# The attention matmuls of 32 and 64 rows in the first block become matmuls of 128 rows

## The chip, the cores and the metric

The kernel runs on one core of a Trainium2 chip. The metric is the device time of one launch in microseconds (us). Before the change three runs gave 2588.17, 2590.54 and 2590.59 us, a median of 2590.54 us.

## The reference, cut to what matters

The reference is a two-block network on 512 tokens of width 1024. The first block mixes three branches; the one that matters here is a sparse attention with 16 query heads of size 64 in 4 key/value groups (4 heads share the keys and values of a group). It has three parts, each with its own gate:

```
s_c = einsum('bghsd,bgnd->bghsn', qh, kc) * scale      # compressed keys: 31 blocks of 32 tokens
o_cmp = einsum('bghsn,bgnd->bghsd', softmax(s_c), vc)  # compressed values
s  = einsum(q, selected keys) * scale                  # 16 blocks can be selected, there are 8: all are
sw = einsum(q, window keys) * scale                    # window 512: all earlier tokens
o  = g0 * o_cmp + g1 * softmax(s) @ v_slc + g2 * softmax(sw) @ v_win
```

`kc` and `vc` come from a small two-layer network over blocks of keys and values. All is float32. The second block (two layers of another attention and a retention) is not touched.

## The kernel before, in words

**Precision.** The matmuls here take operands of the type `F32R`, which are rounded when they are written. So each operand is held in two parts, a rounded "hi" and the rest "lo", and a product is hi\*hi + hi\*lo + lo\*hi: three matmuls that add into one PSUM bank. ScalarE (ACT) writes hi parts, VectorE (DVE) or GpSimd (POOL) the lo parts. Weights stream from HBM in slabs of 8 tiles (128x128), which ACT rounds (`w_hi`) and POOL subtracts (`w_lo`).

**Orders.** Every engine walks the same Python program (`walk`), in which each engine's class implements only its own steps; a step that an engine does not have is `nothing`. So each engine's order of instructions is fixed when the program is written, and semaphore waits join them. Nothing is planned by cost.

**The stage of the change.** The attention is done in 32 sub-units, `SUBS` (L1613): pair of groups `gp` (2), block `i` of 128 queries (4), pair of heads `pp` (2), and `odd` (2), which says which group of the pair is meant. The head size is 64, so two groups lie in one tile of 128 partitions: the even group in rows 0 to 63 and the odd one in rows 64 to 127. The loop in `walk` runs 34 rounds. In round u it weaves, by fixed ratios (`weave`):

- `scores(u)`: four score products (`qk`, head h and branch br), 128\*(i+1) keys wide. DVE takes each out of its bank with the mask and the row minimum (`least`), ACT does the exponentials (`exps`), DVE and POOL the weights.
- `cmp_scores`: the compressed scores and their softmax, once for each block of queries.
- `values`: two rounds behind the scores, the transposed weights (`turn`), split by ACT (`pt_hi`) and DVE (`pt_lo`), then the products with the values (`times`). At a sub-unit's end `cmp_times` adds the compressed part to the same bank, and `out_high`, `out_add`, `out_split` take the result out into `Yhi` and `Ylo`.
- a filler of ordinary products with streamed weights: first the second pair's keys, values and queries (`groups(1)`), then a gate (`branch_gates`).

Six PSUM banks (`spots`) go round among these parts in order of release, two are the filler's.

**The two pairs.** In `qk`, the keys of a group stand in `KS` as 128 rows: the hi part in the group's own 64 rows and the lo part in the other 64. `twice` lets ACT copy the 64 rows of the hi queries into both halves of `QQ`. The first matmul, `QQ` with `KS`, has 128 rows and gives q_hi\*k_hi + q_hi\*k_lo. The second takes the group's own 64 rows of `Ylo` and of `KS` and adds q_lo\*k_hi. `KS` is what streams, and the queries are the loaded weights. In `cmp_times`, the compressed values of a group stand in 32 rows of `vc`, hi beside lo in its 128 columns; two matmuls of 32 rows each take them with the hi and with the lo part of the compressed weights (`ct_hi`, `ct_lo`, each 64 rows: 32 for each group). A row of the trace for line L1714 is a matmul of `mm`, for L1939 an ACT copy or activation of `put`, for L2233 a DVE two-operand instruction; the tiles tell which.

Of the kernel before, what the change touches and what calls it, by code (L numbers as in the profile page):

```python
# [31 lines left out]
R0 = 72  # L32
# [61 lines left out]
def f(ap):  # L94
    return ap.bitcast(F32)
# [76 lines left out]
def program(nc, A, out):  # L172
# [46 lines left out]
    vc = at("vc", R0 + 134, [64, 2, 128], F32R)  # L219
# [8 lines left out]
    Yhi = at("Yhi", R0, [128, KT, 512], F32R)  # L228
    Ylo = at("Ylo", R0 + 16, [128, KT, 512], F32R)
# [13 lines left out]
    QQ = [at(f"QQ{i}", 32 + i, [128, 2, 128], F32R) for i in range(2)]  # L243
# [5 lines left out]
    ct_hi = [at(f"ct_hi{i}", R0 + 130 + 2 * i, [64, 256], F32R) for i in range(2)]  # L249
    ct_lo = [at(f"ct_lo{i}", R0 + 131 + 2 * i, [64, 256], F32R) for i in range(2)]  # L250
    ov = [at(f"ov{i}", 34 + i, [128, 2, 128]) for i in range(2)]
# [120 lines left out]
    class Order:  # L372
# [536 lines left out]
        def cmp_turned(self, gp, i, pp):  # L909
# [3 lines left out]
            self.low(("ct", v), b, banks[b][0:64, 0:256], ct_hi[v % 2][:, :], ct_lo[v % 2][:, :],  # L913
# [796 lines left out]
    class Pe(Order):  # L1710
# [103 lines left out]
        def qk(self, u, n, b, bank_free):  # L1814
            gp, i, pp, odd = SUBS[u]
            h, br = n // 2, n % 2
            width, rows, j = 128 * (i + 1), slice(64 * odd, 64 * odd + 64), 4 * gp + 2 * pp + h
            self.wait_ge(act_nsa.by("twice", u), dve_kqv.by("k", gp, br), bank_free)
            self.mm(banks[b][:, 0:width], QQ[u % 2][:, h, :], KS[gp][odd][:, br, 0:width], True, False)
            self.wait_ge(dve_kqv.by("q", j))  # L1820
            self.mm(banks[b][:, 0:width], Ylo[rows, j, 128 * i:128 * i + 128], KS[gp][odd][rows, br, 0:width], False, True).then_inc(
                *scored(u, n))
# [18 lines left out]
        def cmp_times(self, u, v, ob):  # L1841
            gp, i, pp, odd = SUBS[u]
            rows, o = slice(32 * odd, 32 * odd + 32), banks[ob][:, 0:256]
            self.wait_ge(act_nsa.by("high", "ct", v), dve_cmp.by("value", 3))
            self.mm(o, vc[rows, gp, :], ct_hi[v % 2][rows, :], False, False)
            self.wait_ge(dve_nsa.by("low", "ct", v))
            names = [("out", u)] + [("ct", v)] * odd
            self.mm(o, vc[rows, gp, :], ct_lo[v % 2][rows, :], False, True).then_inc(*valued.named(*names))
# [86 lines left out]
    class Act(Order):  # L1935
# [109 lines left out]
        def twice(self, u, spare_free):  # L2045
            gp, i, pp, odd = SUBS[u]
            j = 4 * gp + 2 * pp
            src = Yhi[64 * odd:64 * odd + 64, j:j + 2, 128 * i:128 * i + 128]
            self.wait_ge(act_kqv.by("q", j + 1), dve_kqv.by("q", j + 1), scored.by(u - 2, 3) if u > 1 else None, spare_free)
            for y in range(2):  # L2050
                ins = self.put(QQ[u % 2][64 * y:64 * y + 64, :, :], src)
# [177 lines left out]
    class Dve(Order):  # L2229
# [97 lines left out]
        def cmp_zero(self):  # L2327
# [665 lines left out]
```

## Time and profile before

| what | value |
|---|---|
| median of three runs | 2590.54 us |
| profiled execution, its own time | 2593.51 us |
| its span, first to last instruction | 2591.7 us |
| PE (TensorE) busy | 2564.2 us, 99% |
| DVE busy | 1157.5 us, 45% |
| ACT busy | 1045.2 us, 40% |
| POOL busy | 1135.2 us, 44% |
| mean granted TensorE clock | 0.994 |
| the attention stage of the change | about 309.6 to 589 us of the span |
| DMA | 250.47 MB, mean 97 GB/s |

A row of the timeline is the start in us, the length in us, the engine, the line, and what was written from what (out<-in). For matmuls "64\*128" is the number of rows (partitions that are summed over) by the columns of the loaded weights, and "64x512" the rows by the streamed columns. A matmul's length is longer than its share of the engine, because matmuls are pipelined: what one costs is the distance from its start to the next one's start. PEld are the weight loads, which can overlap PE. In a wait the engine named behind `<-` released it.

### The profile page before, as it was taken

To read this page: it belongs to the slowest core of one execution; us is meant where nothing else is said; L and a number is where in the kernel's file an instruction comes from. 1 tells how busy PE (TensorE), PEld (TensorE's weight loads), DVE (VectorE), ACT (ScalarE), POOL (GpSimd) and SP (SyncE) were. 2 spreads that over 40 slices of the span, in tenths; PEclk is the share of its full clock that TensorE was granted. 3 is DMA by queue.
4 is the path that set the end of the run, shared out by engine and by line. 5 is a ranking of instruction groups with operands and counts; after the bars stand their busy time and mean duration, and the time that the engine had idled before them with its cause. 6 is when DMAs were issued, how large, how long until landed. Compare 5 with 4: busy or idle time off the path is not lost.

```text
span 2591.7 us, 33239 instructions
## 1 busy us (share of the span) xinstructions
PE 2564.2 (99%) x13376; PEld 2170.9 (84%) x13376; DVE 1157.5 (45%) x2373; ACT 1045.2 (40%) x2006; POOL 1135.2 (44%) x663
## 2 busy tenths in 40 slices
PE   8999999999999999999999999999999999999998
PEld 8888877778888888889888888888898888888887
DVE  6572466556432694101333354542142345544313
ACT  3462376763234433223443333333243333333322
POOL 3354344444445455445344444444444444444342
PEclk9999999999999999999999999999999999999999
DMA  5133210105533354223222222222222222222222
GB/s 189 66 102 105 72 33 25 34 25 195 195 106 138 109 192 167 96 95 105 78 82 82 82 80 83 86 86 98 98 99 88 83 84 79 88 82 83 96 94 87
DMA packets 71769, 250.47 MB, mean 97 GB/s; under 512 B 7872, under 2 KB 12736, under 8 KB 71232
## 3 DMA queue, kind: packets, MB, share of 16 engines
q1 hardware_dynamic: 71616, 248.35, 28.4%
q8 instruction: 106, 1.74, 0.3%
q14 instruction: 47, 0.39, 0.0%
HBM read 246.22 MB, written 2.10 MB: 96 GB/s over the span
## 4 chain that ended last, share of the span: by engine, by line
PE 93%; DVE 4%; ACT 2%; DMA 0%; issue 0%; POOL 0%; DVEq 0%; SPq 0%
PE bank L1714 91%; PE bank L1724 3%; DVE XC L2241 1%; DVE rk_lo L2233 0%; DVE Ylo L2233 0%; DVE sq L2233 0%; ACT TR L1939 0%; ACT w_hi L1939 0%; DVE nt L2233 0%; DMA w_raw<-in_wa 0%; DVE Hlo L2233 0%; DVE nB L2233 0%; ACT Hhi L1939 0%; DMA XR<-in_x 0%; DVE blkk L2237 0%
## 5 line engine op out<-in xcount | busy, mean ns | idle before, releaser
L2769 POOL TENSOR_TENSOR w_lo<-w_raw,w_hi 128x1024 fp32r<-128x1024 f32 (+1 forms) x398 | 949.6, 2390 | 1137.7 <-ACT w_hi L1939 1137.3
L1714 PE MATMUL bank<-Hhi,w_hi 128*128 128x512 f32 (+1 forms) x2144 | 844.0, 394 | 1.4 <-DVE XC L2241 1.3
L1714 PE MATMUL bank<-Hlo,w_hi 128*128 128x512 f32 (+1 forms) x2144 | 825.0, 385 | 2.2 <-DVE Hlo L2233 0.8
L1714 PE MATMUL bank<-Hhi,w_lo 128*128 128x512 f32 (+1 forms) x2144 | 824.2, 384 | 0.0
L1939 ACT ACTIVATE w_hi<-w_raw 128x1024 fp32r<-128x1024 f32 (+1 forms) x398 | 408.0, 1029 | 163.1 <-DMA w_raw<-in_wa 118.1
L1714 PEld LDWEIGHTS bank<-Hhi,w_lo 128*128 128x128 f32 x2144 | 404.5, 189 | 81.3
L1714 PEld LDWEIGHTS bank<-Hhi,w_hi 128*128 128x128 f32 x2144 | 405.1, 189 | 79.8 <-issue 5.3
L1714 PEld LDWEIGHTS bank<-Hlo,w_hi 128*128 128x128 f32 x2144 | 405.5, 189 | 72.3 <-DVE Hlo L2233 3.0
L1714 PE MATMUL bank<-w_hi,Hhi 128*128 128x256 f32 (+2 forms) x384 | 117.6, 306 | 0.0
L1714 PE MATMUL bank<-w_hi,Hlo 128*128 128x256 f32 (+2 forms) x384 | 116.0, 302 | 0.0
L1714 PE MATMUL bank<-w_lo,Hhi 128*128 128x256 f32 (+2 forms) x384 | 115.9, 302 | 0.0
L2794 POOL TENSOR_SCALAR PP<-PP,small 128x128 f32<-128x128 f32 (+3 forms) x128 | 66.1, 536 | 105.5 <-DVE small L2233 105.1
L2506 DVE CUSTOM_DVE_ANT_0 wm<-wm,c 128x1024 f32<-128x1024 f32 x48 | 78.9, 1647 | 9.5 <-DMA wm<-in_w_ada 9.3
L1714 PEld LDWEIGHTS bank<-w_hi,Hhi 128*128 128x128 f32 x384 | 73.0, 190 | 4.4
L1714 PE MATMUL bank<-Fhi,w_hi 128*128 128x512 f32 (+1 forms) x220 | 76.5, 348 | 0.0
L2476 DVE CUSTOM_DVE_ANT_0 PP<-bank,tri 128x128 f32<-128x128 f32 (+3 forms) x128 | 60.5, 487 | 35.7 <-PE bank L1714 34.9
L1714 PE MATMUL bank<-Flo,w_hi 128*128 128x512 f32 (+1 forms) x220 | 76.2, 347 | 0.0
L1714 PE MATMUL bank<-Fhi,w_lo 128*128 128x512 f32 (+1 forms) x220 | 76.2, 347 | 0.0
L1714 PEld LDWEIGHTS bank<-w_lo,Hhi 128*128 128x128 f32 x384 | 73.1, 190 | 3.1
L1939 ACT ACTIVATE PP<-PP,small 128x128 f32<-128x128 f32 (+3 forms) x128 | 70.6, 554 | 11.8 <-DVE small L2476 10.9
L1714 PE MATMUL bank<-Ylo,w_hi 128*128 128x512 f32 x192 | 74.8, 390 | 0.4 <-DVE Ylo L2233 0.4
L1714 PEld LDWEIGHTS bank<-w_hi,Hlo 128*128 128x128 f32 x384 | 73.1, 190 | 2.4
(355 smaller groups left out, 4264.6 us busy)
## 6 DMA issues: line engine op xcount, KB each, us to landing
w_raw<-in_wb SPq DMA_DIRECT2D x211, 512.0 KB, 3.4
w_raw<-in_wa SPq DMA_DIRECT2D x174, 512.0 KB, 3.4
wm<-in_w_ada SPq DMA_DIRECT2D x48, 512.0 KB, 4.4
wa_raw<-in_wb SPq DMA_DIRECT2D x5, 512.0 KB, 6.0
XR<-in_x SPq DMA_DIRECT2D x4, 512.0 KB, 6.5
w1k<-in_w1k SPq DMA_DIRECT2D x1, 2048.0 KB, 12.8
w1v<-in_w1v SPq DMA_DIRECT2D x1, 2048.0 KB, 17.7
XR<-in_x SPq DMA_DIRECT2D x1, 2048.0 KB, 8.3
```

Of the source, the lines that this page charges most:

```text
L1714: return self.e.matmul(o, lhs, rhs, start=start, stop=stop)
L1724: return self.e.transpose(o, i, ident[0:n, 0:n])
L1939: return self.e.activation(o, a, func, **kw)
L2241: return self.e.scalar_tensor_tensor(out=o, in0=a, scalar=s, in1=b, op0=op0, op1=op1)
L2476: self.e.tensor_tensor_reduce(PP[slot][:, n // 2, n % 2, 0:width], banks[b][:, 0:width], tri[:, 512 - width:512], -.125, 3e38, ALU.add, AL ...
L2506: self.e.tensor_tensor_reduce(x, x, cc[l][:, :], .5, 0., ALU.mult, ALU.add, mod[:, l, n:n + 1]).then_inc(*dve_mod("row", l, n))
L2769: self.e.tensor_tensor(x.lo[:, k:k + n, :], x.raw[:, k:k + n, :], f(x.hi[:, k:k + n, :]), ALU.subtract).then_inc(*w_rest(s, k))
L2794: self.e.tensor_scalar(p, p, r[:, n:n + 1], 1., ALU.mult, ALU.mult).then_inc(*pool_nsa("p", u, n))
```

## The change: what it does

- `QQ` gets a second plane: `twice` now copies the hi and the lo rests of the queries (`Y2` is `Yhi` and `Ylo` as one tile), each into both halves, with the same two ACT instructions, each twice as long in elements. The second matmul of `qk` takes `QQ[.., 1, ..]` with all 128 rows of `KS`, so it adds q_lo\*k_hi + q_lo\*k_lo.
- `ct_hi` and `ct_lo` become the two halves (rows 0 to 63 and 64 to 127) of one tile `ct`. `vc` becomes 128 rows for each group: hi and lo values in the group's 32 rows and again 64 rows below, zero elsewhere. `cmp_times` is one matmul of 128 rows, which waits for both parts of `ct`.
- `cmp_zero` clears `vc` too (one memset more), and `cmp_values` copies each group's 32 rows to their second place (four copies more).
- `ov`, `vc`, `QQ` and `ct` move in SBUF; to make room the program asks for 2048 bytes of dynamic DMA scratch in place of the default.

```diff
-    vc = at("vc", R0 + 134, [64, 2, 128], F32R)
+    vc = at("vc", R0 + 136, [128, 2, 2, 128], F32R)
...
-    Yhi = at("Yhi", R0, [128, KT, 512], F32R)
-    Ylo = at("Ylo", R0 + 16, [128, KT, 512], F32R)
+    Y2 = at("Y2", R0, [128, 2, KT, 512], F32R)
+    Yhi, Ylo = Y2[:, 0, :, :], Y2[:, 1, :, :]
...
-    QQ = [at(f"QQ{i}", 32 + i, [128, 2, 128], F32R) for i in range(2)]
+    QQ = [at(f"QQ{i}", 32 + 2 * i, [128, 2, 2, 128], F32R) for i in range(2)]
...
-    ct_hi = [at(f"ct_hi{i}", R0 + 130 + 2 * i, [64, 256], F32R) for i in range(2)]
-    ct_lo = [at(f"ct_lo{i}", R0 + 131 + 2 * i, [64, 256], F32R) for i in range(2)]
-    ov = [at(f"ov{i}", 34 + i, [128, 2, 128]) for i in range(2)]
+    ct = [at(f"ct{i}", R0 + 130 + i, [128, 256], F32R) for i in range(2)]
+    ov = [at(f"ov{i}", R0 + 132 + i, [128, 2, 128]) for i in range(2)]
...
         def qk(self, u, n, b, bank_free):
             gp, i, pp, odd = SUBS[u]
-            h, br = n // 2, n % 2
-            width, rows, j = 128 * (i + 1), slice(64 * odd, 64 * odd + 64), 4 * gp + 2 * pp + h
+            h, br, width = n // 2, n % 2, 128 * (i + 1)
             self.wait_ge(act_nsa.by("twice", u), dve_kqv.by("k", gp, br), bank_free)
-            self.mm(banks[b][:, 0:width], QQ[u % 2][:, h, :], KS[gp][odd][:, br, 0:width], True, False)
-            self.wait_ge(dve_kqv.by("q", j))
-            self.mm(banks[b][:, 0:width], Ylo[rows, j, 128 * i:128 * i + 128], KS[gp][odd][rows, br, 0:width], False, True).then_inc(
-                *scored(u, n))
+            self.mm(banks[b][:, 0:width], QQ[u % 2][:, 0, h, :], KS[gp][odd][:, br, 0:width], True, False)
+            self.mm(banks[b][:, 0:width], QQ[u % 2][:, 1, h, :], KS[gp][odd][:, br, 0:width], False, True).then_inc(*scored(u, n))
...
         def cmp_times(self, u, v, ob):
             gp, i, pp, odd = SUBS[u]
-            rows, o = slice(32 * odd, 32 * odd + 32), banks[ob][:, 0:256]
-            self.wait_ge(act_nsa.by("high", "ct", v), dve_cmp.by("value", 3))
-            self.mm(o, vc[rows, gp, :], ct_hi[v % 2][rows, :], False, False)
-            self.wait_ge(dve_nsa.by("low", "ct", v))
             names = [("out", u)] + [("ct", v)] * odd
-            self.mm(o, vc[rows, gp, :], ct_lo[v % 2][rows, :], False, True).then_inc(*valued.named(*names))
+            self.wait_ge(act_nsa.by("high", "ct", v), dve_nsa.by("low", "ct", v), dve_cmp.by("value", 3))
+            self.mm(banks[ob][:, 0:256], vc[:, gp, odd, :], ct[v % 2][:, :], False, True).then_inc(*valued.named(*names))
...
-            src = Yhi[64 * odd:64 * odd + 64, j:j + 2, 128 * i:128 * i + 128]
+            src = Y2[64 * odd:64 * odd + 64, :, j:j + 2, 128 * i:128 * i + 128]
             self.wait_ge(act_kqv.by("q", j + 1), dve_kqv.by("q", j + 1), scored.by(u - 2, 3) if u > 1 else None, spare_free)
             for y in range(2):
-                ins = self.put(QQ[u % 2][64 * y:64 * y + 64, :, :], src)
+                ins = self.put(QQ[u % 2][64 * y:64 * y + 64, :, :, :], src)
...
         def cmp_zero(self):
+            self.e.memset(f(vc[:, :, :, :]), 0.0)
             self.e.memset(f(kc[:, :, :]), 0.0).then_inc(*dve_cmp("zero"))
...
             for g in range(4):
-                dst, o = vc[32 * (g % 2):32 * (g % 2) + 32, g // 2, :], banks[b][0:32, 64 * g:64 * g + 64]
+                a, o = 32 * (g % 2), banks[b][0:32, 64 * g:64 * g + 64]
+                dst = vc[a:a + 32, g // 2, g % 2, :]
                 self.e.tensor_copy(dst[:, 0:64], o).then_inc(*dve_cmp("value high", g))
                 self.wait_ge(dve_cmp.now())
-                self.tt(dst[:, 64:128], o, f(dst[:, 0:64]), ALU.subtract).then_inc(*dve_cmp("value", g))
+                self.tt(dst[:, 64:128], o, f(dst[:, 0:64]), ALU.subtract).then_inc(*dve_cmp("value low", g))
+                self.wait_ge(dve_cmp.now())
+                self.e.tensor_copy(vc[64 + a:96 + a, g // 2, g % 2, :], dst).then_inc(*dve_cmp("value", g))
...
-    nc = _bacc.Bacc("TRN2", target_bir_lowering=False, num_devices=1)
+    nc = _bacc.Bacc("TRN2", target_bir_lowering=False, num_devices=1, dynamic_dma_scratch_size=2048)
```

## Rows read from the trace of the kernel before

**Rows 1.** The page: busy time of the engines, and the DMA queue.

```profile
PE 2564.2 (99%) x13376; PEld 2170.9 (84%) x13376; DVE 1157.5 (45%) x2373; ACT 1045.2 (40%) x2006; POOL 1135.2 (44%) x663
...
q1 hardware_dynamic: 71616, 248.35, 28.4%
```

**Rows 2.** Stretches: from:to length, busy us of PE, PEld, DVE, ACT, POOL, clock, DMA.

```profile
309.60:394.89 85.29, 85.29 (x466) 65.36 (x464) 53.79 (x181) 63.80 (x172) 39.16 (x58) 1.00 0.11 38
394.89:464.33 69.44, 69.44 (x381) 52.32 (x379) 43.66 (x132) 48.40 (x125) 28.85 (x44) 1.00 0.08 24
464.33:495.22 30.89, 30.89 (x152) 22.53 (x151) 17.59 (x61) 23.20 (x63) 14.05 (x21) 1.00 0.11 36
495.22:589.00 93.78, 93.44 (x499) 68.88 (x499) 55.27 (x143) 62.71 (x144) 37.43 (x46) 1.00 0.10 34
```

**Rows 3.** All waits of PE from 300 to 592 us: total, times, longest.

```profile
PE bank L1714 <- DVE pt_lo L2233: 0.3, 1, 0.3
```

**Rows 4.** PE's timeline, 395 to 404 us.

```profile
395.60 0.49 PE L1714 MATMUL bank<-KS,QQ 128*128 128x512 f32 x1
396.02 0.50 PE L1714 MATMUL bank<-KS,Ylo 64*128 64x512 f32 x1
396.45 0.33 PE L1714 MATMUL bank<-kc,Yhi 128*128 128x128 f32 x1
...
397.47 0.40 PE L1714 MATMUL bank<-Hhi,w_lo 128*128 128x512 f32 x1
397.70 0.39 PE L1714 MATMUL bank<-KS,QQ 128*128 128x512 f32 x1
...
402.29 0.28 PE L1714 MATMUL bank<-pt_hi,VS 128*128 128x256 f32 x1
402.41 0.28 PE L1714 MATMUL bank<-pt_lo,VS 128*128 128x256 f32 x1
402.62 0.38 PE L1714 MATMUL bank<-ct_hi,vc 32*128 32x256 f32 x1
402.85 0.27 PE L1714 MATMUL bank<-ct_lo,vc 32*128 32x256 f32 x1
...
403.39 0.39 PE L1714 MATMUL bank<-Hlo,w_hi 128*128 128x512 f32 x1
```

**Rows 5.** PE's timeline, 445 to 446 us: a narrow score pair and what follows it.

```profile
445.45 0.33 PE L1714 MATMUL bank<-KS,QQ 128*128 128x128 f32 x1
...
445.96 0.33 PE L1724 MATMUL bank<-ident,PP 128*128 128x128 f32 x1
```

**Rows 6.** Weight loads' timeline, 399 to 401 us.

```profile
399.93 0.18 PEld L1714 LDWEIGHTS bank<-KS,Ylo 64*128 64x128 f32 x1 [0.26 <-issue]
400.36 0.19 PEld L1714 LDWEIGHTS bank<-kc,Yhi 128*128 128x128 f32 x1 [0.25 <-issue]
```

**Rows 7.** ACT's groups by shape, 309.6 to 589 us: xcount, busy us, mean ns, idle before.

```profile
L1939 ACT ACTIVATE QQ<-Yhi 64x256 fp32r<-64x256 f32 x60 | 24.8, 413 | 1.1 <-issue 0.3
L1939 ACT ACTIVATE PP<-PP,small 128x512 f32<-128x512 f32 x32 | 22.8, 715 | 2.4 <-DVE small L2476 2.2
...
L1939 ACT ACTIVATE PP<-PP,small 128x256 f32<-128x256 f32 x32 | 16.0, 500 | 3.5 <-DVE small L2476 2.9
```

**Rows 8.** ACT's longest waits, 309.6 to 589 us: total, times, longest.

```profile
ACT pt_hi L1939 <- PE bank L1724: 27.8, 27, 2.7
ACT PP L1939 <- DVE small L2476: 10.9, 18, 1.3
...
ACT C L1939 <- DVE C L2233: 9.2, 6, 2.8
```

**Rows 9.** DVE's timeline, 98 to 108 us.

```profile
101.96 0.20 DVE L2349 CAST vc<-bank 32x64 fp32r<-32x64 f32 x1
...
105.53 0.81 DVE L2238 TENSOR_SCALAR XC<-bank,par 128x512 f32<-128x512 f32 x1 [1.64 <-PE bank L1714]
```

**Rows 10.** A stretch at a lower granted clock, columns as in rows 2.

```profile
1231.80:1242.00 10.20, 10.20 (x48) 10.20 (x48) 6.07 (x15) 4.39 (x10) 3.28 (x4) 0.50 0.01 4
```

More of the change, by code:

```diff
@@ L912, in cmp_turned @@
             v = 2 * (4 * gp + i) + pp
-            self.low(("ct", v), b, banks[b][0:64, 0:256], ct_hi[v % 2][:, :], ct_lo[v % 2][:, :],
+            self.low(("ct", v), b, banks[b][0:64, 0:256], ct[v % 2][0:64, :], ct[v % 2][64:128, :],
                      turned_.by("ct", v), valued.by("ct", v - 2) if v > 1 else None)
@@ L2345, in cmp_values @@
         def cmp_values(self, b, bank_free):
-            self.wait_ge(cmp_sums.by("value"), act_norm.by("h", "first", KT - 1, 1), pool_norm.by("rest", "first", KT - 1, 1))
+            self.wait_ge(cmp_sums.by("value"), dve_cmp.by("zero"), act_norm.by("h", "first", KT - 1, 1), pool_norm.by("rest", "first", KT - 1, 1))
             for g in range(4):
-                dst, o = vc[32 * (g % 2):32 * (g % 2) + 32, g // 2, :], banks[b][0:32, 64 * g:64 * g + 64]
+                a, o = 32 * (g % 2), banks[b][0:32, 64 * g:64 * g + 64]
+                dst = vc[a:a + 32, g // 2, g % 2, :]
                 self.e.tensor_copy(dst[:, 0:64], o).then_inc(*dve_cmp("value high", g))
                 self.wait_ge(dve_cmp.now())
-                self.tt(dst[:, 64:128], o, f(dst[:, 0:64]), ALU.subtract).then_inc(*dve_cmp("value", g))
+                self.tt(dst[:, 64:128], o, f(dst[:, 0:64]), ALU.subtract).then_inc(*dve_cmp("value low", g))
+                self.wait_ge(dve_cmp.now())
+                self.e.tensor_copy(vc[64 + a:96 + a, g // 2, g % 2, :], dst).then_inc(*dve_cmp("value", g))
         def conv(self, j, o, done):
```

## The prediction

> **What bounds the kernel now.** I began with the page's busy times: PE is busy 2564.2 of 2591.7 us, the next engine 45% [rows 1]. Whatever shortens PE's own work shortens the kernel, as long as another engine doesn't take over. So the second view was the stretches of the attention stage, 309.6 to 589 us. In each PE is busy all the time, ACT 63.8 of 85.3, 48.4 of 69.4, 23.2 of 30.9 and 62.7 of 93.8 us, DVE less than ACT, POOL less than half [rows 2]. PE's waits in the stage come to 0.3 us in all [rows 3]. The reader is to see two things: PE's stream is what the stage lasts, and ACT, at 70 to 75% of it, is the next bound and not far off.
>
> The third view was PE's timeline, where a matmul's cost is the distance between starts. A 512-column matmul of 128 rows costs 0.23 us (397.47 to 397.70), a 256-column one 0.12 us (402.29 to 402.41) [rows 4]. A score pair at 512 columns (`QQ`, then `Ylo` with 64 rows) costs 396.45 - 395.60 = 0.85 us, where two plain ones would take 0.46. The weight loads show why: the load for the 64-row matmul starts 0.26 us late, at its matmul's own start, and the next 128-row load is again 0.25 us late [rows 6]. Loads usually run under the matmul before. Here, with a change in the number of rows, each load waits until the array is through, on the way in and on the way out.
>
> **The change part by part, on PE.**
>
> *Score pairs at 256 to 512 columns.* 0.85 - 0.46 = 0.39 us each. I take the same for 256 and 384 columns, since what is lost is the hidden load and not time by column. There are 32 sub-units of four pairs, and three of four blocks of queries are this wide: 96 x 0.39 = 37.4 us.
>
> *Score pairs at 128 columns.* They take 445.96 - 445.45 = 0.51 us [rows 5]. Plain ones cannot cost more than a 256-column one (0.12), nor less than half of it (0.06), so the saving lies between 0.27 and 0.39 us. I take 0.27, because a weight load takes longer than 128 columns stream, and so sets the pace: 32 x 0.27 = 8.6 us.
>
> *Compressed values.* From `pt_lo` at 402.41 to `Hlo` at 403.39 are 0.98 us [rows 4]. With one 128-row matmul of 256 columns there would be 0.12 + 0.12 + 0.23 = 0.47. That saves 0.51 us, 32 times: 16.3 us. Of it 0.12 us is the matmul that goes, the rest the late loads.
>
> PE's work shrinks by 37.4 + 8.6 + 16.3 = 62.3 us. All of it lies on the path, for now.
>
> **On ACT.** `twice` copies 64 x 512 elements where it copied 64 x 256, at 413 ns. Such a copy isn't in the trace at that shape. Exponentials, also SBUF to SBUF, take 715 ns at 512 and 500 at 256 elements per partition [rows 7], so 256 more cost 215 ns. The bounds are 0 (if the fixed part were all) and 413 ns (if it were proportional). I take 215, as the nearest rows are the same engine and the same memory. In the four stretches there are 22, 16, 8 and 14 such copies, 60 in all [rows 7]: 12.9 us more for ACT. Queued behind a longer `twice` are `pt_hi` and the exponentials.
>
> **Which engine ends a stretch then.** For each stretch, PE after the savings against ACT after the addition [rows 2]:
> - 309.6 to 394.9: 16 narrow and 32 wide score pairs, 9 compressed products (they come two rounds behind). PE 85.3 - 4.3 - 12.5 - 4.6 = 63.9; ACT 63.8 + 4.7 = 68.5. ACT is the longer.
> - 394.9 to 464.3: 16 narrow, 16 wide, 7 compressed. PE 69.4 - 4.3 - 6.2 - 3.6 = 55.3; ACT 48.4 + 3.4 = 51.8. PE.
> - 464.3 to 495.2: 16 wide, 5 compressed. PE 30.9 - 6.2 - 2.6 = 22.1; ACT 23.2 + 1.7 = 24.9. ACT.
> - 495.2 to 589: 32 wide, 11 compressed. PE 93.8 - 12.5 - 5.6 = 75.7; ACT 62.7 + 3.0 = 65.7. PE.
>
> The longer of each: 68.5 + 55.3 + 24.9 + 75.7 = 224.4 us in place of 279.4. That is 55.0 us less, 7.3 short of PE's own saving.
>
> An engine that becomes the bound isn't busy without a break. ACT's waits for PE (27.8 us before `pt_hi`, the largest) will go, since PE runs ahead. Its waits for DVE lie inside a chain: 10.9 us for the last row minimum and 9.2 us in the compressed softmax [rows 8]. Between nothing and all 20.1 us of these can come on top. They count only where ACT ends the stretch, 116.2 of 279.4 us of today's time: 20.1 x 0.416 = 8.4 us, and that I take. The saving is 55.0 - 8.4 = 46.6 us.
>
> **Small parts.** `cmp_values` gains four copies in DVE's queue, each about 0.20 us [rows 9] and a semaphore's turn, 1.0 us. DVE then idles 1.64 us before the next product of the convolution [rows 9], which hides them; without that cover they would cost at most 1.0 us. The memset of `vc` is one DVE instruction; PE has work queued there, and I count it at nothing, at most 0.5 us. `cmp_times` waits for the lo part one matmul earlier. Queued behind it on PE is everything, but the lo part is made a few rounds' steps ahead, and PE has no wait on it today [rows 3]. The moved tiles change no instruction. The DMA scratch can only matter to a queue that uses it, and the traffic is in the hardware queue q1, 248.35 MB [rows 1]: nothing. No DMA is added or moved.
>
> **The sum.** The profiled execution took 2593.5 us (span 2591.7 and 1.8 around it). 2593.5 - 46.6 = 2546.9. It lay 3.0 us above the median of the runs, so against the median: 2544 us.
>
> **The rivals.**
>
> *ACT takes over for good.* Bank turnover couples the engines: six banks go round, and each is freed by DVE behind ACT. If a saturated ACT delays the releases, PE waits in stretches that I gave to PE. For it: ACT at 94% of the second stretch and 87% of the fourth, by the sums above. Against: PE shows no such wait today. Price: all 20.1 us of chain waits come back and 5 us in each PE stretch: 55.0 - 20.1 - 10 = 25 us saved, 2566 us.
>
> *PE stays the bound.* The copy costs nothing more and ACT keeps ahead. The first stretch has ACT 63.8 against PE 63.9, so it would just do. Then all 62.3 us come: 2528 us.
>
> *Rows don't matter.* The loads would be late for another reason, such as the change of the streamed tile. The Trainium skill has a rule that says so: "TensorE: Matmul & The Clock Gate", section "Why this matters for your kernels", gives a single matmul of 32 rows the same time as one of 128. By it only the dropped matmul counts, 32 x 0.12 = 3.8 us, 2587 us. By this rule the change would be worth hardly anything; the trace disagrees at every switch (0.12 us for 256 columns of 128 rows, 0.23 for 32 rows [rows 4]), but it shows them only in company. That `kc` after `Ylo` also loads late [rows 6], with 128 rows and another streamed tile, speaks a little for this rival; that `pt_hi` follows `pt_lo` at 0.12 speaks against it.
>
> *Slower: the clock.* Where ACT becomes the bound PE idles between matmuls. In this trace there is a stretch at a granted clock of 0.50 (the 1.2 GHz level), where 48 matmuls took 10.2 us, 0.21 each, mostly of 256 columns [rows 10], against 0.12 at the full clock [rows 4]: 78% more. If the first and third stretch (86 us of PE work) ran so, it would add 67 us, less the 7 us in which ACT is the longer anyway: 2544 + 60 = 2604 us. It decides from about 67 us of PE's work at that level. Against it: the clock is 1.00 throughout [rows 2], and the waits expected are short and scattered.
>
> **How the numbers follow.** The forecast 74%, ACT for good 12%, PE all the way 8%, rows don't matter 3%, the clock 3%. The forecast's own range is from the copy at 0 or 413 ns and the chain waits at 0 or 20.1 us: 2533 to 2560. The range reaches toward both neighbours: 2530 to 2566. A time within 0.2% of 2590.5 us (5 us) can't be told from no change. Faster by more than that: 94%, and most of "rows don't matter" falls within it: 3% same, 3% slower.
>
> **What would show it.** Each step has its sign in the changed profile. Score pairs at 512 columns cost 0.46 us from start to start and no weight load there is late; if they still cost 0.85, the third rival holds. One `vc` matmul of 128 rows in 0.12 us. The `QQ` copy near 630 ns. PE begins to wait for DVE or ACT in the first and third stretch, some 5 to 15 us in all, and the stretches last about 75, 55, 27 and 76 us. The forecast is wrong if PE's waits exceed 25 us, or if the time saved isn't in this stage.

## The result and the profile after

Four runs of the changed kernel gave 2547.46 to 2553.03 us, median 2548.35; four of the kernel before 2588.17 to 2590.59, median 2590.37. The ratio is 0.9843, interval [0.9826, 0.986]: 42 us faster. The forecast was 2544 us, in the range of 2530 to 2566.

The profiled execution took 2548.61 us, 44.9 less than before's. Against its own time the forecast was 2546.9: 1.7 us off.

The page, busy times and DMA queue (answers to [rows 1]), and from its fourth part the chain of what ended last, by engine:

```profile
PE 2505.4 (98%) x13344; PEld 2156.1 (85%) x13344; DVE 1158.3 (45%) x2378; ACT 1053.6 (41%) x2006; POOL 1135.1 (45%) x663
...
q1 hardware_dynamic: 71616, 248.35, 29.1%
...
PE 87%; DVE 6%; ACT 5%; issue 1%; DMA 0%; POOL 0%; DVEq 0%; SPq 0%; ACTq 0%
```

PE lost 58.8 us of busy time and 32 matmuls. ACT's instructions are as many as before and its busy time is 8.4 us longer; in the stage the longer copies alone are 12.9 us, which the part on the prediction comes back to. DVE has five more instructions. DMA moves the same.

The stage by the same four sub-unit groups as [rows 2]: from:to length, busy us of PE, PEld, DVE, ACT, POOL, clock, DMA share, GB/s:

```profile
311.41:382.33 70.92, 66.02 (x456) 59.95 (x455) 51.45 (x177) 64.92 (x168) 37.86 (x56) 1.00 0.14 46
382.33:443.00 60.67, 57.23 (x373) 49.52 (x372) 43.56 (x135) 52.59 (x129) 28.74 (x42) 1.00 0.09 27
443.00:467.61 24.61, 23.17 (x147) 19.89 (x146) 17.41 (x60) 23.01 (x60) 14.63 (x22) 1.00 0.13 44
467.61:546.80 79.19, 77.14 (x490) 67.14 (x489) 53.76 (x146) 65.36 (x148) 38.45 (x48) 1.00 0.13 41
```

The stage lasts 235.4 us in place of 279.4: 44.0 of the 44.9 us. PE and the length now differ, by 4.9, 3.4, 1.4 and 2.1 us. ACT is busy for 92% of the first stretch and 94% of the third, and PE for 93% and 94%: neither fills them.

All waits of PE from 300 to 560 us (answers to [rows 3]): total, times, longest:

```profile
PE bank L1713 <- DVE pt_lo L2226: 4.1, 4, 2.6
PE bank L1723 <- DVE pt_lo L2226: 2.5, 3, 1.1
PE bank L1723 <- POOL PP L2791: 2.1, 3, 1.4
PE bank L1713 <- DVE ct L2226: 1.6, 3, 0.7
PE bank L1723 <- POOL C L2783: 1.0, 1, 1.0
PE bank L1723 <- DVE small L2473: 0.3, 1, 0.3
```

They come to 11.6 us. Nearly all are at the free end of a bank: PE waits until DVE or POOL has taken something out. None names ACT, though ACT is busier than DVE and POOL: where `pt_lo` frees the bank it stands one step further back, since DVE subtracts from the bank what ACT rounded out of it (`pt_hi`).

PE's timeline (answers to [rows 4]; `x4` is four matmuls drawn as one row):

```profile
389.47 0.28 PE L1713 MATMUL bank<-pt_lo,VS 128*128 128x256 f32 x1
389.59 0.28 PE L1713 MATMUL bank<-ct,vc 128*128 128x256 f32 x1
389.70 0.40 PE L1713 MATMUL bank<-Hhi,w_hi 128*128 128x512 f32 x1
389.94 0.40 PE L1713 MATMUL bank<-Hlo,w_hi 128*128 128x512 f32 x1
...
391.31 1.09 PE L1713 MATMUL bank<-KS,QQ 128*128 128x512 f32 x4
392.24 0.39 PE L1713 MATMUL bank<-Hhi,w_hi 128*128 128x512 f32 x1
```

Two score pairs at 512 columns take 392.24 - 391.31 = 0.93 us, 0.465 each; the forecast said 0.46. The compressed product itself costs 389.70 - 389.59 = 0.11 us, and from the `pt_lo` ahead of it to `Hlo` are 389.94 - 389.47 = 0.47 us, the value forecast, in place of 0.98 [rows 4].

The weight loads at the same place (answers to [rows 6]) have no idle time in front:

```profile
391.20 0.78 PEld L1713 LDWEIGHTS bank<-KS,QQ 128*128 128x128 f32 x4
392.02 0.19 PEld L1713 LDWEIGHTS bank<-Hhi,w_hi 128*128 128x128 f32 x1
```

ACT's group of the copy (answers to [rows 7]) gives mean 628 ns, the value forecast:

```profile
L1932 ACT ACTIVATE QQ<-Y 64x512 fp32r<-64x512 f32 x60 | 37.7, 628 | 1.1 <-issue 0.3
```

ACT's three chain waits in the stage (answers to [rows 8]):

```profile
ACT pt_hi L1932 <- PE bank L1723: 8.5, 11, 1.5
ACT C L1932 <- DVE C L2226: 7.3, 6, 2.8
ACT PP L1932 <- DVE small L2473: 4.1, 9, 1.2
```

The wait for PE fell from 27.8 to 8.5 us; it did not go. The waits for DVE fell from 20.1 to 11.4.

**Outside the stage** little moved. The added copies in `cmp_values` (answers to [rows 9]), DVE, then POOL at the same time:

```profile
105.85 2.03 DVE L2348 CAST vc<-vc 32x128 fp32r<-32x128 f32 x1
...
108.41 0.22 DVE L2348 CAST vc<-vc 32x128 fp32r<-32x128 f32 x1
...
105.41 2.39 POOL L2766 TENSOR_TENSOR w_lo<-w_raw,w_hi 128x1024 fp32r<-128x1024 f32 x1 [10.63 <-ACT w_hi L1932]
```

Three of the four copies took 0.22 us, the third of them in order 2.03. It began while POOL's `w_lo` ran and ended just behind it. The experiments meet this again.

### The profile page after: what moved, and what is told of

It is laid out like the page before. It is cut to its first block, busy times and chain, and to the rows that moved or that the text cites. A ratio compares the mean times of both kernels' runs of the same rounds, so it can differ in the third digit from the quotient of the medians.

```text
span 2546.8 us, 33180 instructions
## 1 busy us (share of the span) xinstructions
PE 2505.4 (98%) x13344; PEld 2156.1 (85%) x13344; DVE 1158.3 (45%) x2378; ACT 1053.6 (41%) x2006; POOL 1135.1 (45%) x663
## 4 chain that ended last, share of the span: by engine, by line
PE 87%; DVE 6%; ACT 5%; issue 1%; DMA 0%; POOL 0%; DVEq 0%; SPq 0%; ACTq 0%
PE bank L1713 85%; PE bank L1723 2%; ACT PP L1932 1%; ACT pt_hi L1932 1%; ACT w_hi L1932 1%; ACT QQ L1932 1%; DVE XC L2234 1%; DVE pt_lo L2226 0%; DVE rk_lo L2226 0%; DVE C L2226 0%; DVE PP L2473 0%; DVE Y L2226 0%; DVE sq L2226 0%; ACT TR L1932 0%; DVE nt L2226 0%
## 5 line engine op out<-in xcount | busy, mean ns | idle before, releaser
L1713 PE MATMUL bank<-Y,w_hi 128*128 128x512 f32 x384 | 118.5, 390 | 0.4 <-DVE Y L2226 0.4
L1713 PEld LDWEIGHTS bank<-Y,w_hi 128*128 128x128 f32 x384 | 72.1, 188 | 15.6 <-DVE Y L2226 0.8
L2503 DVE CUSTOM_DVE_ANT_0 wm<-wm,c 128x1024 f32<-128x1024 f32 x48 | 79.1, 1651 | 9.8 <-DMA wm<-in_w_ada 9.5
L1713 PE MATMUL bank<-Y,w_lo 128*128 128x512 f32 x192 | 74.8, 390 | 0.0
```

Of the source, the lines that this page charges most:

```text
L1713: return self.e.matmul(o, lhs, rhs, start=start, stop=stop)
L2503: self.e.tensor_tensor_reduce(x, x, cc[l][:, :], .5, 0., ALU.mult, ALU.add, mod[:, l, n:n + 1]).then_inc(*dve_mod("row", l, n))
```

## The experiments

In this table stand the stage's four stretches, cut at the same sub-units in each kernel, PE's busy time and recorded waits in it, and the median of the runs with the ratio to the kernel before, run on the same chip. The profile rows behind it have the form of [rows 2] and [rows 3]. The kernel before was run anew beside each group of experiments, with medians of 2590.37 to 2592.01 us, while the changed kernel was run only for the result above. So a difference of one or two us between rows of the median column may be that of the occasion; the ratio takes it out, and the stage's length, read from the traces, is the finer measure.

| kernel | stretches, us | stage | PE busy | PE waits | median, us | ratio |
|---|---|---|---|---|---|---|
| before | 85.3 69.4 30.9 93.8 | 279.4 | 279.1 | 0.3 | 2590.37 | |
| after | 70.9 60.7 24.6 79.2 | 235.4 | 223.6 | 11.6 | 2548.35 | 0.9843 [0.9826, 0.986] |
| e1, scores only | 72.3 61.1 24.9 81.8 | 240.2 | 235.6 | 4.5 | 2552.48 | 0.985 [0.9835, 0.9864] |
| e2, values only | 80.8 66.1 28.4 88.4 | 263.7 | 263.4 | 0.3 | 2575.07 | 0.994 [0.9925, 0.9955] |
| e3, short copy | 69.9 58.7 23.8 78.3 | 230.6 | 222.3 | 7.8 | 2543.58 | 0.9815 [0.9801, 0.983] |
| e5, second copy on DVE | 75.9 60.1 24.0 79.0 | 238.9 | 225.1 | 13.6 | 2553.27 | 0.9851 [0.9834, 0.9867] |
| e6, DMA scratch only | 85.3 69.4 30.9 93.8 | 279.4 | 279.1 | 0.3 | 2590.04 | 0.9995 [0.9986, 1.0005] |
| e7, both of a pair 64 rows | 80.3 66.4 28.9 91.5 | 267.1 | 266.8 | 0.3 | 2578.34, one run | |
| e8, copies made twice | 82.9 67.2 27.9 87.8 | 265.8 | 232.5 | 32.5 | 2576.61 | 0.9951 [0.9934, 0.9968] |
| e9, DVE copy from 12, late memset | 76.0 59.6 24.0 79.0 | 238.5 | 225.6 | 12.8 | 2547.89 | 0.9834 [0.9819, 0.9849] |
| e10, later keys, late memset | 70.1 60.7 24.6 79.1 | 234.4 | 223.2 | 11.2 | 2545.62 | 0.982 [0.9807, 0.9833] |
| e11, e9 and e10 | 74.0 59.6 24.0 78.9 | 236.5 | 223.8 | 12.6 | 2546.61 | 0.9826 [0.9813, 0.9839] |
| e12, e11 with the copy from 13 | 70.1 61.4 24.0 79.0 | 234.5 | 223.1 | 11.3 | 2546.4 | 0.9824 [0.9811, 0.9838] |

### The two halves of the change

e1 is the kernel before with the score pairs of the change alone:

```diff
-            self.mm(banks[b][:, 0:width], Ylo[rows, j, 128 * i:128 * i + 128], KS[gp][odd][rows, br, 0:width], False, True).then_inc(
-                *scored(u, n))
...
+            self.mm(banks[b][:, 0:width], QQ[u % 2][:, 1, h, :], KS[gp][odd][:, br, 0:width], False, True).then_inc(*scored(u, n))
...
+                ins = self.put(QQ[u % 2][64 * y:64 * y + 64, :, :, :], src)
```

> Only the score pairs change (queries' hi and lo both held twice, second score matmul over 128 rows); the compressed product keeps its two 32-row matmuls. Theory (late weight loads at a change of rows, ACT the next bound): PE's own saving is 46 us, with ACT as long as PE in the first and third stretch some 4 to 8 us of it is lost in waits, so 38 to 42 us less than before, 2548 to 2552 us, and adding the compressed part on top is worth only a few us. Rival (rows don't matter): within 2 us of before. Rival (parts simply add, PE bound throughout): 31 us less, three quarters of the measured 42, 2559 us.

e2 is the kernel before with the compressed values alone:

```diff
-            self.mm(o, vc[rows, gp, :], ct_hi[v % 2][rows, :], False, False)
-            self.wait_ge(dve_nsa.by("low", "ct", v))
-            self.mm(o, vc[rows, gp, :], ct_lo[v % 2][rows, :], False, True).then_inc(*valued.named(*names))
+            self.mm(banks[ob][:, 0:256], vc[:, gp, odd, :], ct[v % 2][:, :], False, True).then_inc(*valued.named(*names))
```

> Only the compressed product changes (one matmul of 128 rows for two of 32), the scores are as before. Theory: PE stays the bound everywhere, so the full 16.3 us comes, less up to 1 us for the added memset: 2574 to 2576 us. Rival (rows don't matter, only the dropped matmul counts): 3.8 us, 2587 us.

(Both also have the 2 KB of DMA scratch, which e6 shows to be free.) e2's stage is 279.4 - 263.7 = 15.7 us shorter, where the prediction had 16.3, and PE waits no more than before (0.3 us). That is an edit of PE alone whose price was read rightly. e1's stage is 39.2 us shorter, PE's busy time 43.5 us less, where the prediction had 46.0; its time, 2552.48 us, is half a microsecond above the expectation. The longest of its waits:

```profile
PE bank L1714 <- DVE pt_lo L2230: 3.0, 2, 2.6
PE bank L1724 <- POOL C L2783: 0.9, 1, 0.9
...
```

One by one the halves save 39.2 + 15.7 = 54.9 us, together 44.0. The 10.9 us between appear only when both are in. PE's busy time explains little of it: 43.5 + 15.7 = 59.2 us one by one, 55.5 together. Even these 3.7 us need not be work: PE's instructions are the same in e3, the changed kernel and e8, and its busy time grows with its waits, 222.3, 223.6 and 232.5 us beside waits of 7.8, 11.6 and 32.5. The loss is the mark of a second bound. With the scores' half in, the first stretch has PE at 69.5 and ACT at 66.3 us (e1); the values' half alone takes 4.5 us off it (e2), and on top of e1 only 1.4.

### What the 64 rows cost

e7 puts both matmuls of a pair on the group's own 64 rows, as neighbours, and leaves q_hi\*k_lo out. All else is the kernel before.

```diff
-            self.mm(banks[b][:, 0:width], QQ[u % 2][:, h, :], KS[gp][odd][:, br, 0:width], True, False)
+            self.mm(banks[b][:, 0:width], QQ[u % 2][rows, h, :], KS[gp][odd][rows, br, 0:width], True, False)
```

> The kernel before, but the first score matmul, too, takes only the group's own 64 rows (q_hi*k_lo is left out), so both of a pair have 64 rows at the same place and the ACT work is as before. Theory (the cost is at the change of the number of rows): inside a pair the distance at 512 columns is the plain 0.23 us and a loss of about 0.3 us stays where the pair is left, so two pairs in a row take 4 x 0.23 + 0.1 and the stage gets shorter than before's 279.4 us by 5 to 25 us. Rival (every matmul of fewer rows has a late load): 0.33 us and more inside a pair, and the stage gets longer than before, by up to 30 us.

PE's timeline of e7, two pairs and what stands around them:

```profile
391.25 0.28 PE L1714 MATMUL bank<-pt_lo,VS 128*128 128x256 f32 x1
391.46 0.49 PE L1714 MATMUL bank<-KS,QQ 64*128 64x512 f32 x1
391.80 0.39 PE L1714 MATMUL bank<-KS,Ylo 64*128 64x512 f32 x1
392.03 0.39 PE L1714 MATMUL bank<-KS,QQ 64*128 64x512 f32 x1
392.27 0.38 PE L1714 MATMUL bank<-KS,Ylo 64*128 64x512 f32 x1
392.58 0.33 PE L1714 MATMUL bank<-kc,Yhi 128*128 128x128 f32 x1
```

Between matmuls of 64 rows the pitch is 0.23 and 0.24 us at 512 columns, as with 128 rows. The extra time stands at the ends: 0.21 (for 0.12) into the first, 0.34 (for 0.23) behind it, 0.31 (for 0.23) out of the last, 0.28 us in sum; the `kc` matmul behind them takes 0.16 to the next start, where in e1, behind 128 rows, it takes 0.06. That makes 0.38 us. So 64 rows by themselves cost nothing; the change of the row count does. And it costs about the same for one such matmul as for four: a single `Ylo` [rows 4] costs 0.09 us ahead of it (397.70 to 398.02, for 0.23), 0.20 itself (0.43 at 396.02) and 0.10 behind. The count agrees: the 128 matmuls of 64 rows each stood alone before, and stand in 99 groups in e7, 29 changes fewer in and out. At 0.39 us that is 11.3 us; the stage is 12.3 us shorter, with the same number of matmuls.

The Trainium skill ("TensorE: Matmul & The Clock Gate", "Why this matters for your kernels") gives one matmul of 32 rows the time of one of 128. For 64 rows, and between matmuls of the same number of rows, e7 agrees: 0.23 us. As a forecast of this change, 2587 us, it was refuted by e2: of 15.7 us saved, only 32 x 0.12 = 3.8 are the dropped matmul. Another page of the Trainium skill, "TensorEngine Tiling (Array Packing)", "Key Properties", says that a change of the tiling mode drains TensorE. The late loads in [rows 6] and the rows above agree with it, and put a size to it, about 0.4 us for in and out.

### What ACT's longer copies cost

e3 keeps the pairs and leaves the copy of the low rests out; the second matmul takes the hi queries again (q_lo\*k_hi is replaced by a second q_hi product). PE's instructions stay the same, and ACT's copies are as short as before.

```diff
-            self.mm(banks[b][:, 0:width], QQ[u % 2][:, 1, h, :], KS[gp][odd][:, br, 0:width], False, True).then_inc(*scored(u, n))
+            self.mm(banks[b][:, 0:width], QQ[u % 2][:, 0, h, :], KS[gp][odd][:, br, 0:width], False, True).then_inc(*scored(u, n))
...
-                ins = self.put(QQ[u % 2][64 * y:64 * y + 64, :, :, :], src)
+                ins = self.put(QQ[u % 2][64 * y:64 * y + 64, 0, :, :], src[:, 0, :, :])
```

> As the changed kernel, but the ACT copies are as short as before (64 x 256 elements) and the second score matmul takes the hi queries a second time, so the lo part of the queries is left out; PE's instructions are the same. Theory (the longer copies on ACT cost part of PE's saving): ACT has 12.9 us less to do, the stage shortens by 4 to 8 us against the changed kernel, 2540 to 2545 us, and PE's waits fall from 11.6 to under 6 us. Rival (PE is the bound, the waits come from chains of bank turnover that don't depend on ACT's load): within 2 us of the changed kernel.

The copy's group in e3, 414 ns again:

```profile
L1932 ACT ACTIVATE QQ<-Y 64x256 fp32r<-64x256 f32 x62 | 25.7, 414 | 1.2 <-issue 0.3
```

The time is in the expected range (2543.58), the stage 4.8 us shorter than the changed kernel's. But 7.8 us of PE's waits remain, more than expected: they are not for the longer copies. The largest is the same as in the changed kernel, 2.6 us in the first stretch.

e8 goes the other way: the changed kernel, with both copies made a second time behind the first.

```diff
                 ins = self.put(QQ[u % 2][64 * y:64 * y + 64, :, :, :], src)
+            ins.then_inc(*act_nsa("once", u))
+            self.wait_ge(act_nsa.now())
+            for y in range(2):
+                ins = self.put(QQ[u % 2][64 * y:64 * y + 64, :, :, :], src)
             ins.then_inc(*act_nsa("twice", u))
```

> The changed kernel, with ACT making both copies of the queries two times, with a wait between, so ACT has 60 x 0.63 = 38 us more in the stage and PE's instructions are the same. Theory (ACT is within a few us of being the bound): ACT's 206 us become 244, which is more than the 235 us that the stage now lasts, so the stage grows to 250 to 260 us and the time by 15 to 25 us, to 2564 to 2573 us. Rival (PE has slack against ACT): less than 8 us more.

e8's stretches, columns as in [rows 2]:

```profile
310.80:393.75 82.95, 69.10 (x457) 59.94 (x456) 51.58 (x177) 78.68 (x190) 38.95 (x58) 1.00 0.12 39
393.75:460.96 67.21, 59.02 (x374) 49.61 (x373) 43.58 (x134) 61.49 (x142) 27.79 (x40) 1.00 0.08 25
460.96:488.87 27.91, 23.76 (x148) 19.79 (x147) 16.19 (x59) 27.29 (x68) 14.05 (x22) 1.00 0.12 39
488.87:576.63 87.76, 80.62 (x490) 66.82 (x489) 54.05 (x147) 75.36 (x167) 38.89 (x49) 1.00 0.11 37
```

ACT gains 242.8 - 205.9 = 36.9 us of work and the stage 30.4: 0.82 us for each. That was above the expectation (2576.61 against 2564 to 2573). The second copies also make the queries ready later, and 4.8 of PE's 32.5 us of waits now name ACT itself, so not all of it is ACT's load. In e3 12.0 us less of ACT's work gave 4.8 us, 0.40 for each. From these two points the changed kernel seems to sit on a bend: ACT is close enough to the end that what is added costs nearly all, and what is taken away gives less than half. Also the fourth stretch grew by 8.6 us with ACT at only 86% of it. An engine need not be full to end a stretch, when it and PE wait for each other in turn.

### Giving the second copy to DVE

In e5, DVE makes one of the two copies, and POOL the memset of `vc`.

```diff
-            for y in range(2):
-                ins = self.put(QQ[u % 2][64 * y:64 * y + 64, :, :, :], src)
-            ins.then_inc(*act_nsa("twice", u))
+            self.put(QQ[u % 2][0:64, :, :, :], src).then_inc(*act_nsa("twice", u))
...
+            self.e.tensor_copy(QQ[u % 2][64:128, :, :, :], f(src)).then_inc(*dve_nsa("twice", u))
```

> As the changed kernel, but the copy into the upper half of the query tile is DVE's instead of ACT's, and the memset of the compressed values is POOL's instead of DVE's. Theory: ACT loses 19 us of work in the stage and DVE gains about 15 to 22 (it stands at 71%), so PE is the bound again: 6 to 10 us less than the changed kernel, 2538 to 2543 us, and the 0.8 us that PE waits more at 77 us of the span goes too. Rival (DVE's longer queue delays the bank releases as much as ACT did): within 2 us of the changed kernel or slower.

It missed: 2553.27 us, with a ratio of 0.9851 against the changed kernel's 0.9843 no faster, and the stage is 3.5 us longer though 17.6 us of work left ACT. All of that is the first stretch, 4.9 us longer; the others are 1.5 us shorter. The median copy on DVE is 424 ns, but the mean 561. Here is the worst one on DVE, and POOL's timeline at that time:

```profile
379.41 2.62 DVE L2228 CAST QQ<-Y 64x512 fp32r<-64x512 f32 x1
382.07 0.56 DVE L2477 CUSTOM_DVE_ANT_0 PP<-bank,tri 128x384 f32<-128x384 f32 x1
...
379.37 2.38 POOL L2773 TENSOR_TENSOR w_lo<-w_raw,w_hi 128x1024 fp32r<-128x1024 f32 x1 [4.50 <-ACT w_hi L1932]
```

POOL began 0.04 us earlier, and DVE's copy ended 0.28 us after POOL did. Every copy over 0.45 us in this trace (seven, of 0.52 to 2.62 us) overlapped an instruction of POOL that had begun before it; so did the 2.03 us `vc` copy of the changed kernel. It goes the other way too. Behind most of the 0.42 us copies POOL began a `PP` instruction some 0.06 us later, and then that one was long: the longest is 0.93 us, in the changed kernel 0.71. The groups of the widest form, changed kernel, then e5:

```profile
L2791 POOL TENSOR_SCALAR PP<-PP,small 128x512 f32<-128x512 f32 x32 | 21.6, 695 | 24.2 <-DVE small L2226 24.2
L2798 POOL TENSOR_SCALAR PP<-PP,small 128x512 f32<-128x512 f32 x32 | 22.9, 739 | 25.2 <-DVE small L2231 25.2
```

In the stage POOL is busy 6.6 us longer than in the changed kernel (126.3 against 119.7). Here the trace agrees with the Trainium skill ("SBUF — State Buffer", "Who interferes with whom"): a DVE copy within SBUF can want the ports that GpSimd uses, and the one that comes second waits for the whole instruction of the other. The minimum-taking DVE instructions behind it then come 2.2 us late, and PE waits for their banks (1.55 us at 382.69). The first stretch also has 3.4 us at half the clock, further ahead (0.98 over the stretch).

e9 hands over the copy only from sub-unit 12 on, so that nearly all of the first stretch stays as it was, and clears `vc` after `cmp_keys`, late enough to be out of the way of the product PE waits for.

```diff
+            if u < 12:
+                return
...
+            self.e.tensor_copy(QQ[u % 2][64:128, :, :, :], f(src)).then_inc(*dve_nsa("twice", u))
...
-            self.e.memset(f(vc[:, :, :, :]), 0.0)
...
+            self.e.memset(f(vc[:, :, :, :]), 0.0).then_inc(*dve_cmp("clear"))
```

> The changed kernel with two amendments: the memset of the compressed values stands behind the compressed keys in DVE's order, where DVE idles 8.6 us, and from sub-unit 12 on DVE makes one of the two query copies (in the first stretch DVE has no room). Theory: 0.8 us less before the stage, and 1.4 us less in the stretches behind sub-unit 12, as those were with DVE copying throughout: 2 us less than the changed kernel, 2546 us. Rival (DVE's queue is as tight as ACT's there): no difference, or slower.

The first copy on DVE fell on a long POOL instruction again, at the end of the first stretch, 2.61 us. PE's row behind it:

```profile
378.92 0.62 PE L1713 MATMUL bank<-KS,QQ 128*128 128x384 f32 x2 [2.45 <-DVE small L2482]
```

Its first stretch is 76.0 us against 70.9. Part is this wait; part is the clock, which the stretch's row gives at 0.96 of full speed, with two episodes of 3.4 us at the half level (1.2 GHz). The stretches' rows separate the two roughly: with the same instructions PE is busy 69.0 us in place of 66.0, and idle 7.0 in place of 4.9. The three later stretches are 1.9 us shorter than the changed kernel's, where 1.4 were expected; the stage is 238.5 against 235.4.

### Moving the low keys

PE's longest wait in the changed kernel has a plain chain. PE, then DVE:

```profile
333.80 0.51 PE L1713 MATMUL bank<-KS,QQ 128*128 128x256 f32 x2 [2.63 <-DVE pt_lo L2226]
...
331.22 1.39 DVE L2226 TENSOR_TENSOR KS<-bank,KS 64x512 fp32r<-64x512 f32 x2 [2.18 <-ACT KS L1932]
332.64 0.18 DVE L2482 RECIPROCAL small<-small 128x4 f32<-128x4 f32 x1
332.86 0.16 DVE L2226 TENSOR_TENSOR small<-small,gate 128x4 f32<-128x4 f32 x1
333.05 0.69 DVE L2226 TENSOR_TENSOR pt_lo<-bank,pt_hi 128x512 fp32r<-128x512 f32 x1
```

DVE stands 2.18 us, waiting for ACT to write the hi keys, with `pt_lo` queued behind; `pt_lo` frees PE's bank. e10 puts the low keys of the second pair three steps later in the weave, and has the late memset:

```diff
                 def low():
+                    if gp:
+                        yield 3
                     self.keys_low(gp, br, o)
```

> The changed kernel with the memset of the compressed values behind the compressed keys, and DVE's subtraction for the second pair's keys three filler steps later in its order. Theory: PE's longest wait in the stage (2.6 us at 331 us of the span) is for a bank that DVE frees behind that subtraction, which itself waits 2.2 us for ACT; with the subtraction later the wait shrinks by 1 to 2 us, and the memset's 0.8 us goes: 2545 to 2547 us. Rival (ACT's queue alone sets that wait): the 2.6 us stay and only 0.8 us is gained.

e10's waits of PE with their rows:

```profile
330.95 0.51 PE L1715 MATMUL bank<-KS,QQ 128*128 128x256 f32 x2 [0.98 <-DVE pt_lo L2228]
337.37 0.50 PE L1715 MATMUL bank<-KS,QQ 128*128 128x256 f32 x2 [1.58 <-DVE ct L2228]
```

2.63 us became 0.98, and the wait six microseconds on grew to 1.58. The stage is 1.0 us shorter, the median 2545.62 the lowest of all kernels that compute the whole reference. Against the changed kernel it is 2.7 us, but the two intervals of the ratios overlap (0.9807 to 0.9833 and 0.9826 to 0.986), so it isn't shown to be faster.

e11 joins e9 and e10, with the DVE copy written as a multiplication by one, to see whether it is the copy's form that stalls.

```diff
+            self.ts(QQ[u % 2][64:128, :, :, :], f(src), 1., None, ALU.mult).then_inc(*dve_nsa("twice", u))
```

> As the run with the later keys, and DVE makes one of the two query copies from sub-unit 12 on, as a multiplication by 1 in place of a copy. Theory: the first DVE copy of this form took 2.61 us in place of 0.42, and PE waited 2.45 us for it and then ran at half the clock for 3.4 us; an instruction form that DVE uses all the time has no such first cost, so the 1.4 us of ACT's relief show: 2543 to 2546 us. Rival: the first one stalls in any form, or DVE's queue costs what ACT's saves: no better than the run without the shared copy.

DVE, then POOL, in e11:

```profile
373.91 2.60 DVE L2241 TENSOR_SCALAR QQ<-Y 64x512 fp32r<-64x512 f32 x1
...
373.88 2.35 POOL L2777 TENSOR_TENSOR w_lo<-w_raw,w_hi 128x1024 fp32r<-128x1024 f32 x1 [5.37 <-ACT w_hi L1934]
```

Form doesn't matter: it stalls as the copy did, 0.03 us after POOL's start. PE then waits 2.4 us for the bank behind it, and runs at the half clock for the next 3.4 us. e12 is e11 with DVE's copies from sub-unit 13 on, which leaves out just the one that met POOL's long subtraction.

```diff
-            if u < 12:
+            if u < 13:
```

> As the run with the later keys and the shared copy, but DVE's copies begin at sub-unit 13 in place of 12. In both runs with DVE copies that began at 12, the first fell 0.04 us behind the start of a 2.35 us subtraction of POOL and ended 0.3 us behind its end. Theory (such a DVE instruction waits for the POOL instruction that is under way): the copy that collided is ACT's again, so no DVE copy in the stage lasts over 1 us, PE's 2.4 us wait goes, the clock stays at 1.00 and the stage lasts 232.5 to 233.5 us in place of 236.5; the time is 2543 to 2545 us. Rival (the first DVE copy is slow wherever it stands): the stall moves to the copy for sub-unit 13 and the stage stays at about 236 us.

The long one is gone (DVE's 19 copies take 419 to 897 ns, median 424), and the first stretch is 70.1 us at a clock of 1.00. The first stretch is 3.9 us shorter than e11's: that shows by removal that the stall made it long, or brought on what did. The second is 1.8 us longer, so the stage gains 2.0 us, and not the 3 to 4 expected. And the kernel gains nothing over e10: stage 234.5 against 234.4, 2546.4 us against 2545.62. ACT has 11.4 us less work (194.5 against 206.0) and it doesn't show. In e3 about the same relief gave 4.8 us; there DVE got no work in exchange (166.1 us busy, here 173.9), and POOL wasn't slowed (120.0, here 123.7). So near balance the work seems to weigh on whichever engine gets it; e3 without the later keys and e12 with them aren't a strict pair.

### The DMA scratch

e6 is the kernel before with the 2 KB scratch.

```diff
-    nc = _bacc.Bacc("TRN2", target_bir_lowering=False, num_devices=1)
+    nc = _bacc.Bacc("TRN2", target_bir_lowering=False, num_devices=1, dynamic_dma_scratch_size=2048)
```

> The kernel before with nothing changed but the 2048 bytes of dynamic DMA scratch. Theory: all transfers are in the hardware queue, so nothing: within 2 us of before. Rival (the scratch or the shifted layout moves the transfers' timing): a difference of over 3 us, and other landing times of the weight slabs than 3.4 us.

Ten runs, 0.9995 [0.9986, 1.0005], the stage unchanged to the tenth: it does nothing to the time. It only makes room.

## Why the prediction was right, and where it was not

**The bound now, and the late loads: right.** The saving is in PE's stream, in this stage, and comes from loads that are no longer late. Compressed product: 16.3 us forecast, 15.7 measured alone (e2). Score pairs: 46.0 forecast, 43.5 of PE's busy time alone (e1). In sum 59.2 of the 62.3 us, 5% less.

The pair that the price was read from was not a typical one: 0.85 us is the second of two pairs in a row, and holds what the first left behind. Over all pairs the mean from start to start was 0.78, 0.69, 0.57 and 0.44 us at 512, 384, 256 and 128 columns before, and 0.47, 0.38, 0.27 and 0.20 in e1. So the price is the same at 256 to 512 columns, as assumed, but in the pair it is 0.30 and not 0.39 us, and 0.24 at 128 columns; that makes about 37 us. The other 7 came in the matmul behind a pair, which the prediction didn't name. Before:

```profile
517.59 0.44 PE L1714 MATMUL bank<-KS,Ylo 64*128 64x384 f32 x1
517.96 0.50 PE L1714 MATMUL bank<-Hhi,w_hi 128*128 128x512 f32 x1
518.30 0.40 PE L1714 MATMUL bank<-Hlo,w_hi 128*128 128x512 f32 x1
```

`Hhi` takes 0.34 us there, and in e1 at the same places 0.24. The two errors nearly cancel.

**The copy on ACT: its length right, its share of ACT's time not.** 215 ns more was the forecast, 628 - 413 = 215 measured. The slope of the exponentials held for the copy. But ACT's busy time in the stage grew by 7.7 us (198.1 to 205.9), where 12.9 were added in the forecast. The number of its instructions is the same and their lengths add up to 12.4 us more (224.5 to 236.9). They overlap each other at their ends, and more of them do so when ACT waits less: 26.4 us of overlap before, 31.0 after, and 30.2 in e3, which has the short copies and is busy for only 193.9 us. To add lengths to a busy time overstates the sum.

**The longer engine of each stretch: the sum right, the stretches off.** Forecast 75, 55, 27 and 76 us, measured 70.9, 60.7, 24.6 and 79.2. The two stretches in which ACT was to end are 6.5 us shorter than forecast, the two of PE 8.9 us longer. These errors cancel to 2.4 us, so part of the good hit is luck. Two steps failed.

The first is that ACT is the longer engine in the first and third stretch, 68.5 and 24.9 us. It is busy for 64.9 and 23.0 us, 5.5 less, for the reason above, and PE for 66.0 and 23.2: the two are level. What ACT is not busy there, 6.0 + 1.6 = 7.6 us, is near the 8.4 that I took for chain waits.

The second is that chain waits "count only where ACT ends the stretch". They count wherever both are close: PE stands idle for 3.4 us in the second stretch with ACT at 87% of it, and e8 shows the fourth growing with ACT at 86%. In all the stage is 235.4 - 223.6 = 11.8 us longer than PE's busy time; I had 8.4 above the longer engine, and in two stretches only.

**PE's waits.** 5 to 15 us were forecast, 11.6 measured. Their place was wrong in part: 4.9 of them lie in the first stretch and 1.5 in the third, 3.4 and 2.0 in the others. And the longer copies aren't their whole cause: 7.8 us stay in e3. A faster PE meets queues that it never had to wait for, as `pt_lo` behind the low keys on DVE.

**Small parts.** The memset and the four copies were forecast to cost nothing to 0.5 us, and the hidden copies at most 1.0. The copies cost DVE 1.8 us more than I counted, since one met POOL; the next product's instruction then comes without the 1.64 us of idle time that [rows 9] shows, and PE has no wait for DVE there. At the stage's start the changed kernel is 1.8 us later than the kernel before (311.4 against 309.6); 1.0 of it arises in the first tens of microseconds, where neither half of the change is at work but the changed kernel's trace is at half the clock for 17.1 us and before's for 10.2. The other part is PE's wait for DVE's `XC` near 76 us: 1.2 to 1.6 us in the kernels without an early memset on DVE, 1.9 to 2.3 with it, but also 1.9 in e5 and 2.1 in e10, where POOL made it or it came late. And the stage's start differs by more than this between kernels without the memset: 308.5 us in e6, 309.6 before, 311.2 in e7. So the memset's price, under a microsecond, isn't settled. The scratch: nothing (e6).

**The rivals.** "Rows don't matter" fell to e2 and e7. "PE all the way", 2528, would need waits near zero; even e3 has 7.8. "ACT for good", 2566, has the right mechanism with too high a price: PE's stretches grew by 8.9 us where it put 10, but ACT's chain waits didn't all come back (11.4 of 20.1 us are left). "The clock": 1.00 in all four stretches, though PE waited up to 2.6 us at a time. In the first stretch of e9, e11 and e5 it did fall, to 0.96, 0.98 and 0.98, in e11 right behind a wait of 2.4 us; so the risk was real and small. The forecast's own range, 2533 to 2560, doesn't follow from the ends it names: with the copy at 0 and no chain waits the same sum gives 2529, with 413 ns and all 20.1 us 2562. The range of 2530 to 2566 covers nearly all of that.

**Against the median.** The forecast took the profiled execution of before to lie 3.0 us above its median and carried that over. After's lay 0.3 above. The stretch at half clock of [rows 10] is missing after the change, and the two traces draw 2.7 us apart there. It is missing in e1, e6, e7 and e8 too, so it comes and goes without the change; a later one of 3.4 us (near 1901 us before, 1855 after) is in both. With the 1.8 us lost ahead of the stage, 44.0 in it and these 2.7, the 44.9 us between the two executions are complete. Of the 4.4 us between 2544 and 2548.35, 2.7 are this difference of the two offsets, and 1.7 the forecast's own error.

## What to carry to other kernels

In a stream of matmuls of 128 rows, one with fewer rows costs late weight loads on its way in and out (here about 0.4 us for both together, part of it in the matmul behind); fill the rows with zeros, copies or a second part of the same product before you count columns. Read such a price from many places, and to the second matmul behind. When the bound engine gets faster, compare it with the next one stretch by stretch, and add something in every stretch where the next is close (here 86% and more), not just where it wins: taking ACT's work away gave 0.4 us for each microsecond, adding to it cost 0.8. Before work moves to DVE, look at what POOL is doing at that time.

## What the runs showed of the hardware that I had not expected

A DVE copy from SBUF to SBUF of 64x512 elements takes 0.42 us, or 2.6 us when it starts 0.03 us behind a POOL subtraction of 2.35 us; as a multiplication by one the same. Small ones too: 32x128 took 0.22 or 2.03 us. When the copy starts first, it is POOL's instruction that lasts longer: up to 0.93 us for one of at most 0.71.

The cost of fewer rows is that of a change, not of a matmul: inside a run of 64-row matmuls the pitch is 0.23 us at 512 columns, as with 128 rows. Part of it, 0.10 us, falls on the matmul behind.

ACT instructions that follow each other without a wait overlap: in the stage their lengths add up to 236.9 us and keep ACT busy for 205.9.
